# Query panels of layer 0 projected in the indexer's score units, modulation panels in the looped attention groups

## What is computed

```
q, k, v, iq, ik, iw = split(h @ w_in);  q, k, iq, ik = rope_partial(...)
dots  = einsum('bqhd,bsd->bqhs', iq, ik)
score = einsum('bqhs,bqh->bqs', relu(dots), iw);  score = where(causal, score, -inf)
top_score, idx = top_k(score, n_sel)
logits = q . k[idx] * HEAD_DIM**-0.5;  p = softmax(logits);  o = p . v[idx]
modulation: m = silu(c) @ w + b, split in shift, scale and gate
```

## Time and profile before

| what | us |
|---|---|
| median of 3 runs (lowest, highest) | 1773.04 (1772.23, 1774.61) |
| the profiled execution, its own time | 1770.04 |
| its span in the profile | 1768.2 |
| PE busy (share of the span), mean granted clock | 1584.4 (90%), 0.918 |
| DVE busy, ACT busy, POOL busy | 808.5, 674.0, 159.4 |

### The profile page before, as it was taken

One profiled execution on the slowest core, in us unless ns is written; L12 is line 12 of the kernel. 1 busy time (PEld: TensorE's weight loads), 2 busy tenths in 40 slices (PEclk: granted clock), 3 DMA queues, 4 the chain that ended last, 5 costly groups with the idle time before them and its releaser, 6 DMA issues.

```text
span 1768.2 us, 30809 instructions
## 1 busy us (share of the span) xinstructions
PE 1584.4 (90%) x12113; PEld 1413.8 (80%) x12113; DVE 808.5 (46%) x1739; ACT 674.0 (38%) x1203; POOL 159.4 (9%) x285
## 2 busy tenths in 40 slices
PE   6889678889888999999899778999798999998996
PEld 4874367678487999999899777777497999997995
DVE  2437956777336333233344524443335344334433
ACT  4424234435215343333333544445225333334334
POOL 0120011101103000000000421111102000000001
PEclk9898588889799999999999989889899999999998
DMA  9335630003542553554232130003632222222211
GB/s 298 95 123 189 216 119 4 21 0 120 194 140 72 191 163 125 186 166 136 94 108 75 32 128 25 24 12 122 242 108 66 96 95 93 78 77 76 85 48 49
DMA packets 154552, 189.79 MB, mean 107 GB/s; under 512 B 6805, under 2 KB 148413, under 8 KB 150166
## 3 DMA queue, kind: packets, MB, share of 16 engines
q1 hardware_dynamic: 144338, 145.77, 25.9%
q0 software_dynamic: 5600, 36.44, 5.5%
q10 hardware_dynamic: 4528, 6.37, 1.1%
HBM read 183.92 MB, written 4.83 MB: 107 GB/s over the span
## 4 chain that ended last, share of the span: by engine, by line
PE 72%; DVE 12%; issue 9%; ACT 4%; DMA 1%; another core or an unknown queue 1%; SPq 1%; DVEq 0%; ACTq 0%; POOL 0%; POOLq 0%
PE ps L537 52%; PE ps L1198 3%; PE ps L1267 2%; DVE arena L1180 2%; PE ps L1249 2%; PE ps L563 2%; DVE small L1179 2%; PE ps L1217 1%; DVE arena L1431 1%; PE ps L1542 1%; PE ps L1488 1%; PE ps L1258 1%; DVE arena L1423 1%; DVE rt L673 1%; ACT arena L1333 1%
## 5 line engine op out<-in xcount | busy, mean ns | idle before, releaser
L537 PE MATMUL ps<-hH,wH 128*128 128x260 f32 x2576 | 531.5, 288 | 45.2 <-DVE hL L721 25.8
L537 PE MATMUL ps<-hH,wL 128*128 128x260 f32 x2576 | 525.6, 286 | 0.0
L537 PE MATMUL ps<-hL,wH 128*128 128x260 f32 x2576 | 525.0, 286 | 0.0
L537 PEld LDWEIGHTS ps<-hH,wH 128*128 128x128 f32 x2576 | 405.3, 192 | 53.8 <-issue 52.4
L521 DVE TENSOR_TENSOR wL<-ring,wH 128x1024 fp32r<-128x1024 f32 (+1 forms) x170 | 203.3, 1199 | 535.0 <-ACT wH L515 534.8
L515 ACT ACTIVATE wH<-ring 128x1024 fp32r<-128x1024 f32 (+1 forms) x182 | 188.5, 1037 | 567.5 <-PE ps L537 554.1
L537 PEld LDWEIGHTS ps<-hL,wH 128*128 128x128 f32 x2576 | 403.8, 192 | 0.0
L537 PEld LDWEIGHTS ps<-hH,wL 128*128 128x128 f32 x2576 | 403.7, 191 | 0.0
L1333 ACT ACTIVATE arena<-arena 128x128 f32<-128x128 f32 (+3 forms) x128 | 72.2, 564 | 187.1 <-DVE arena L1417 103.1
L1249 PE MATMUL ps<-arena 80*128 (+4 forms) x256 | 102.4, 491 | 6.7 <-DVE arena L1314 2.6
L1267 PE MATMUL ps<-arena 128*128 (+1 forms) x640 | 91.2, 276 | 14.4 <-ACT arena L1341 14.0
(11 more groups left out here) (273 smaller groups left out, 1796.0 us busy)
## 6 DMA issues: line engine op xcount, KB each, us to landing
ring<-in_w_ada SPq DMA_DIRECT2D x48, 1024.0 KB, 7.7
ring<-in_w_up SPq DMA_DIRECT2D x44, 1024.0 KB, 5.2
ring<-in_w_down SPq DMA_DIRECT2D x16, 1024.0 KB, 5.1
ring<-in_w_in_a SPq DMA_DIRECT2D x8, 1024.0 KB, 7.3
ring<-in_w_down SPq DMA_DIRECT2D x8, 768.0 KB, 4.6
ring<-in_w_in_b SPq DMA_DIRECT2D x6, 1024.0 KB, 5.6
ring<-in_w_o_a SPq DMA_DIRECT2D x4, 1024.0 KB, 9.3
ring<-in_w_o_b SPq DMA_DIRECT2D x4, 1024.0 KB, 11.3
```

Of the source, the lines that this page charges most:

```text
L537: ins = pe.matmul(ps[:, 2 * p + half, 0:HT], w[:, h, kc, t * P:t * P + P], mov[:, k0 + kc, half * HT:half * HT + HT], start=(first and kc ...
```

## The change

The section "q0" of the ring becomes four panels in slots 3 and 0 and is loaded ahead of "ada0b", which becomes three times six panels, all in slot 3. Panel 0 of the queries is projected in the score units 1 to 4 and 6 to 9, two parts of six matmuls in each, in banks 2 and 3; panels 1 to 3 follow behind the units, around the samples' score. ACT splits and copies in the score stage too, the copies going to `sq` (panel 0) and to the rows of `OT` that the attention's output takes later; POOL makes all eight low halves. In the looped groups the parts, splits and copies go; six modulation panels stand in units 0, 3, 6, 10, 13 and 17 (bank 7), with their turns in the next unit (bank 6), and the rotations in units 8 and 15. The panels in units 10 and 17 wait for the rope to have read banks 6 and 7. Layer 1 is as before.

```diff
-            ("ada0b", [(s, W) for s in ((3, 0, 1, 3, 0) + (2, 1, 3, 0) * 4)[:NSC]], 1),
-            ("q0", [(3, W)], 4),
+            ("q0", [(s, W) for s in (3, 0, 3, 0)], 1),
+            ("ada0b", [(3, W)] * NPL, 3),
...
+        FIRST_Q = {u: (2 * (u - 1), 2 * (u - 1) + 1) for u in (1, 2, 3, 4)}
+        FIRST_Q.update({u: (2 * (u - 2), 2 * (u - 2) + 1) for u in (6, 7, 8, 9)})
...
+            def queries(j, h, pairs):
+                half_ready(pe, "q0", 0, j, h)
+                mm_half(pe, h, pairs, HK * h, HK, h == 0, h == 1, mid="at_mm" if h else None)
...
                 (turn if op == "turn" else dots)(b)
-                if u % 3 == 2:
-                    pe_panel(pe, u // 3)
+                for part in FIRST_Q.get(u, ()):
+                    pe_qpart(pe, "q0", 0, 0, part, 1)
             for op, b in SAMPLE_OPS[NPAIR:]:
                 (turn if op == "turn" else dots)(b)
-            pe_panel(pe, NPAIR // 3)
...
-            pe_panel(pe, NPAIR // 3 + 1)
+            pe.wait_ge(S("at_raw"), 2)
+            pe.wait_ge(S("sk_evac"), NS + 1)
+            queries(1, 0, (1, 2))
...
-            for x in range(NPAIR // 3 + 2, NSC + 1):
-                pe_panel(pe, x)
+            queries(1, 1, (1, 2))
+            pe.wait_ge(S("sk_scs"), 2)
+            for h in range(2):
+                queries(2, h, (3, 0))
+            pe.wait_ge(S("at_raw"), 4)
+            for h in range(2):
+                queries(3, h, (1, 2))
...
-                if u % 3 == 2:
-                    act_panel(act, u // 3)
+                if u < 2:
+                    split_high(act, "q0", 0, 0, u)
+                if u in (5, 10):
+                    query(0, u // 10, 1)
+                if u in (8, 11):
+                    split_high(act, "q0", 0, 1, u // 11)
...
+            pool.wait_ge(S("sk_qz"), 1)
+            for j in range(4):
+                for h in range(2):
+                    split_low(pool, "q0", 0, j, h)
...
+        PANEL_AT = (0, 3, 6, 10, 13, 17)
+        ROTATE_AT = (8, 15)
+
+        def pe_hosted(pe, g, n, u):
+
+            x = g * NPL + 8
+            if u in PANEL_AT:
+                j = PANEL_AT.index(u)
+                if j == 3:
+                    pe.wait_ge(S("at_pair"), n * 2 + 4)
+                if j == 5:
+                    pe.wait_ge(S("at_pair"), n * 2 + 5)
+                ada_panel(pe, "ada0b", g, j, 7)
+            if u - 1 in PANEL_AT:
+                j = PANEL_AT.index(u - 1)
+                pe.wait_ge(S("ad_out"), x + j)
+                ada_turn(pe, x + j, j, 6)
+            if u in ROTATE_AT:
+                pe.wait_ge(S("ad_out"), x + (3, 5)[u // 15])
+                pe_qrot(pe, g + 1, n + 1, u // 15)
...
+                if nxt is not None and l == 0:
+                    pe_hosted(pe, g, n, u)
+                elif nxt is not None:
                     for part in QPARTS.get(u, ()):
-                        pe_qpart(pe, f"q{l}", nxt, n + 1, part)
-                    if l == 0 and u in (8, 16):
-                        pe_qrot(pe, n + 1, u // 16)
+                        pe_qpart(pe, "q1", nxt, n + 1, part)
...
             for t in range(2):
-                for part in range(8):
-                    pe_qpart(pe, f"q{l}", 0, n0, 8 * t + part)
                 if l == 0:
-                    pe_qrot(pe, n0, t)
+                    pe_qrot(pe, None, n0, t)
+                else:
+                    for part in range(8):
+                        pe_qpart(pe, "q1", 0, n0, 8 * t + part)
...
-                        if l == 0 and u in (9, 17):
-                            rope(n + 1, u // 17)
+                        if l == 0 and u in (9, 16):
+                            rope(nxt, n + 1, u // 16)
...
             if l == 0:
-                for h in range(2):
-                    split_low(dve, "q0", 0, 0, h)
                 for t in range(2):
-                    rope(n0, t)
+                    rope(None, n0, t)
```

More of the change, by code:

```diff
@@ L1111, in keys, with query @@
                 act.activation(ikb[:, b % 2, :], ps[:, 4, :], ACT.Copy).then_inc(S("sk_evac"), 1)
+            def query(j, t, p):
+                if t == 0:
+                    act.wait_ge(S("at_mm"), j + 1)
+                else:
+                    act.wait_ge(S("w_used"), used("q0", 0, j))
+                act.activation(v520(q_raw(2 * j + t) if j else sq[:, t, :]), pair(p), ACT.Copy).then_inc(S("at_raw"), 1)
             for u in range(NPAIR):
@@ L1187, in build, with q_raw, pe_qpart @@
         QPAIR = 3
-        def pe_qpart(pe, sec, i, n, part):
+        def q_raw(t):
+            return OT[:, ds(t, 1), :].rearrange("p o t -> p (o t)")
+        def pe_qpart(pe, sec, i, n, part, pair_no=3):
             t, h, kc = part // 8, part // HK % 2, part % HK
-            if h + kc == 0:
+            if h + kc == 0 and sec == "q1":
                 pe.wait_ge(S("at_pair"), n * 2 + (t + 1))
+            elif part == 8:
+                pe.wait_ge(S("at_raw"), 1)
             if t == 0 and kc == 0:
@@ L1197, in pe_qpart @@
                 for half in range(2):
-                    ins = pe.matmul(ps[:, 2 * QPAIR + half, 0:HT], w[:, h, kc, t * P:t * P + P],
+                    ins = pe.matmul(ps[:, 2 * pair_no + half, 0:HT], w[:, h, kc, t * P:t * P + P],
                                     mov[:, HK * h + kc, half * HT:half * HT + HT],
@@ L1205, in pe_qpart, with q_source, pe_qrot, act_hosted @@
                     ins.then_inc(S("at_mm"), 1)
-        def pe_qrot(pe, n, t):
-            pe.wait_ge(S("at_raw"), n * 2 + (t + 1))
+        def q_source(g, t):
+            return q_raw(g * 2 + t) if g is not None else sq[:, t, :]
+        def pe_qrot(pe, g, n, t):
+            pe.wait_ge(S("at_pair"), n * 2 + (t + 1))
             for half in range(2):
-                ins = pe.matmul(ps[:, 2 * QPAIR + half, 0:HT], swap, raw2[:, t, half * HT:half * HT + HT], start=True, stop=True)
+                ins = pe.matmul(ps[:, 2 * QPAIR + half, 0:HT], swap, q_source(g, t)[:, half * HT:half * HT + HT], start=True, stop=True)
             ins.then_inc(S("at_rot"), 1)
+        PANEL_AT = (0, 3, 6, 10, 13, 17)
[16 more added lines that the diff above has]
+                pe_qrot(pe, g + 1, n + 1, u // 15)
+        def act_hosted(act, g, u):
+            if u in PANEL_AT:
+                j = PANEL_AT.index(u)
+                ada_row(act, "ada0b", g, j, j, 7)
+            if u - 1 in PANEL_AT:
+                ada_result(act, g * NPL + (8 + PANEL_AT.index(u - 1)), 6)
         def pe_turn(pe, pages, c, bank):
@@ L1341, in units @@
                         act.activation(PT[:, v % 2, 0:w], ps[:, 2 + v % 2, 0:w], ACT.Copy).then_inc(S("at_pt"), 1)
-                    if nxt is not None:
+                    if nxt is not None and l == 0:
+                        act_hosted(act, g, u)
+                    elif nxt is not None:
                         if u < 2:
```

85 lines of the change are left out of this document (39 added, 46 removed).

## The result

The changed kernel takes 1785.25 us (median of 14 runs, 1774.67 to 1789.55) against 1771.99 for the kernel before in the same runs: a ratio of 1.0072, 95% interval 1.0060 to 1.0084. The forecast was 1760.5 with a range to 1777: wrong, in sign too. The profiled execution after has a span of 1783.1 us (before: 1768.2).

A forecast was written before the change was run, and what follows sets the result against it. PE was taken to bound the score units, DVE the top-k, with PE's clock deciding in the groups. 10.5 - 15.4 - 7.5 = -12.4 took the profiled 1770.04 to 1757.6; with 3.0 to the median, 1760.5 us, range 1748 to 1777.

The forecast's parts named there:

- Score units: Before the top-k: panel 0's parts, the split wait and smaller terms delay the top-k by 10.5 us (8.5 to 13).
- the two uncertain terms: Score units: POOL's split blocking DVE's last sums, 0 to 2.35 us; clock fall in the wait, up to 1.7.
- Rival B: POOL's splits stop the top-k, five falling on it, 11.7 us: no change, 1772; 0.18 shared with two other cases.
- Prologue: From the top-k's mask to group 0's first unit: only rotations left, 8.6 us instead of 23.97, so -15.4.
- Rival D: Under the top-k: panels 1 to 3 run cold, end 8 us late: 1768; 0.18 shared with two other cases.
- rival C: Clock up from unit 4, second wait short: -5 us a group, 8.5 in score units: 1750; chance 0.10.
- Looped groups: Three looped groups of layer 0: panels and turns replace projection matmuls, -2.5 us a group, -7.5 in all.
- clock up between units 7 and 9: Looped groups: the forecast's main case, PE's clock rises between these units and is 1.00 from unit 10; chance 0.55.
- (a): Looped groups, units 0 to 9: panels and reload cost, lost parts gain; unit 10 starts 0.9 us earlier to 3 later.
- the rope: Looped groups, units 9 and 10: S product now ahead of the bank wait, DVE starts unit 10 earlier, -2.3 us.
- (c): Looped groups, unit 15 to next group: earlier rotation spares DVE's wait, ACT places after the last panel: -0.4 us.
- rival A: Looped groups: clock stays at 0.50 without the projection parts, groups 58 to 60 us, 1789 to 1795; chance 0.17.

The follow-up runs named there:

- e7: Changed kernel with all four query projections and six of 18 modulation panels under the top-k, four panels and 53 fillers per looped group: 1736.21 us, ratio 0.9808.
- e1: Changed kernel plus 42 filling matmuls, results never read, in every looped group of layer 0: 1767.69 us, ratio 0.9984 against the kernel before.

## Why the prediction was wrong, step by step

**Score units, +10.5 forecast, +13.0 measured, +1.4 more in the top-k.** The mechanism was right. First to last dots grew by 10.9 us (25.31 to 36.23): 1.97 is the wait for the split (2.1 forecast), and with 7.1 for the parts, which is the forecast's own figure, 1.8 remain for the fall of the clock that I had priced at up to 1.7 (0.50 from 140 to 143 us, PE busy 3.00 of 3.00). Of the two uncertain terms, 2.35 and 1.7, I had taken 1.3 together; both came nearly in full. The term that was mis-sized is the splits' hold on DVE: 2.0 at the last addition and 1.3 in the first mask. Rival B named the mechanism and the wrong victim: MAX8 and the replacing were not touched, the addition and the mask were. The Trainium skill, SBUF — State Buffer, section "SBUF: two separate sides", has the pair of ports held for a whole instruction against a DVE operation with two SBUF inputs or in a two-port mode; the addition, with two inputs (2.73 us beside a split of 2.34), agrees with it. The mask, with one input (1.63 beside 2.40), agrees only if it ran in such a mode, which no row names.

**Prologue, -15.4 forecast, -15.4 measured.** 8.61 us against 8.6, with both rotations cold at 2.07 and 2.10 us, and the projections ran under the top-k at the full clock (1.00 from 175 to 211 us) and ended there. Rival D did not come. (Three slips in the working changed nothing: 288 matmuls at half clock are 61.9 us by the earlier trace rows, not 62.5; the parts of rival C add up to 1751, not 1750; and half of the 0.18 is 0.09, less than the 0.13 counted for no change.)

**Looped groups, -7.5 forecast, +9.9 measured: the step that failed.** The forecast rested on "clock up between units 7 and 9" and "the clock 1.00 from there". The first came: in each group PE was cold for some 17 us, and unit 7 starts after 17.3, 18.0 and 18.8. The second failed, at about unit 12 of each group. By stretches of a group, from the starts of DVE's units (for group 1 the rows below, with the earlier trace rows):

| stretch | before, group 1 | after, groups 0, 1, 2 | forecast |
|---|---|---|---|
| unit 0 to unit 9 | 19.52 | 21.43, 22.16, 22.92 | (a): -0.9 to +3 |
| unit 9 to unit 10 | 6.21 | 4.16, 4.16, 4.16 | the rope: -2.3 |
| unit 10 to unit 15 | 15.82 | 15.55, 17.19, 19.16 | with the row above: -3.5 |
| unit 15 to the next group | 9.63 | 9.98, 9.94, 12.75 | (c): -0.4 |

```profile
316.45 0.55 DVE L1413 CUSTOM_DVE_ANT_0 arena<-ps,arena 128x384 f32<-128x384 f32 x1 [0.41 <-issue]
```

```profile
319.07 0.55 DVE L1472 CUSTOM_DVE_ANT_0 arena<-ps,arena 128x384 f32<-128x384 f32 x1 [0.48 <-issue]
...
323.24 0.56 DVE L1472 CUSTOM_DVE_ANT_0 arena<-ps,arena 128x384 f32<-128x384 f32 x1
...
340.43 0.69 DVE L1472 CUSTOM_DVE_ANT_0 arena<-ps,arena 128x512 f32<-128x512 f32 x1
```

So the rope's gain came nearly in full, 2.05 in every group, and (a) used it up: it came at the late end of its range though the rise was not late. From unit 10 on, where the gain was to be, groups 1 and 2 lost, group 2 the most, where the clock took longest to come back. The parts in units 9 to 14, which the change took out, were what ran while it came back in the kernel before. That is rival A, which I gave 0.17, but in another form than I wrote: not a clock that never rises, but one that falls in the middle of a group and is then long in coming back. It fell some microseconds behind two short waits of PE, of panel 3 for the rope and of the products for the outputs (group 1 of the kernel after):

```profile
322.37 1.07 PE L567 MATMUL ps<-ring,cT 128*32 128x256 f32 x16 [0.82 <-DVE rt L1431]
...
325.72 0.88 PE L1323 MATMUL ps<-arena 128*128 x6 [1.11 <-DVE arena L1447]
```

But the same two waits stand in group 1 of e7, where the clock is 1.00 throughout:

```profile
304.39 1.07 PE L571 MATMUL ps<-ring,cT 128*32 128x256 f32 x16 [0.82 <-DVE rt L1454]
...
307.75 0.88 PE L1342 MATMUL ps<-arena 128*128 x6 [1.11 <-DVE arena L1470]
```

So these waits alone do not bring it down, and what does stays open. I had taken it as a fact that units with 384 and 512 keys "keep PE busy by themselves" and so would raise it. The row 382 to 402 says otherwise, and I had the earlier trace rows before me: 40.48 busy of 41 us at 0.50. The row that I set against A, the score units at 0.92, had its rise before the first panel came (1.00 from 135 us on, the panel at 136.39); that the clock stays up through panels was no sign that it rises on them. And group 3, which has four filling matmuls in every unit, ran at 0.99 in the same table.

**The reload wait** was forecast as some 3 us ahead of panel 1. It is 0.7 to 1.3 us at panels 0 and 1, five waits, 5.1 us in all three groups. Those at panel 0, 1.20 and 1.31 in groups 1 and 2, were not forecast and are part of what (a) took.

**Group 3, forecast unchanged, +3.2.** It starts at 409.37, where the clock, 1.00 since 403, had just fallen; its mean is 0.91 (0.99 before). I had called it untouched, which its code is; the clock that it inherits is not. In e1 it takes 35.0 again.

**The sum.** The forecast was -12.4 for the profiled execution, and +14.9 came: 27.3 apart, of which the front is 3.9 (+13.0 + 1.4 - 15.4 = -1.0 for -4.9), the groups 17.4, group 3 3.2, and 2.9 lie in stages of the same code, ahead of the score units and behind group 3.

## What to carry to other kernels

Before a dense piece of matmul work is moved out of a stage, look at what the granted clock does in that stage: where it rises on that piece, taking it out also makes what stands behind it dearer (a panel took 1.93 us at 0.50 and 1.07 at 1.00). Work that replaces it has to be tried for that, not counted in microseconds; a few filling matmuls are cheap to try (three lines gave 0.5% on the kernel before). And work moved off a long path belongs under the longest wait, not between the steps of a stage that the same engine bounds: all four projections fitted under the top-k, and the one in the score units cost what the move had gained.
